# Two transformer blocks on one core: norms tile by tile over both halves, and first pieces summed with the feature tile outermost

## What is computed

```python
def rmsnorm(x, g):
    y = xf * lax.rsqrt(jnp.mean(xf * xf, axis=-1, keepdims=True) + EPS)
    return (y * g).astype(x.dtype)
def adaln(x, g, shift, scale):
    return rmsnorm(x, g) * (1 + scale) + shift
...
h = _rmsnorm(x, mix_norm_even[i]);  h @ w_in_even[i]
hx = adaln(x, norm1_g[layer], mod_x[0], mod_x[1]); hc = adaln(ctx, norm1_g[layer], mod_c[0], mod_c[1])
... hx @ w_in; hc @ w_in ...
swiglu(h, w1, w3, w2) = (silu(h @ w1) * (h @ w3)) @ w2
```

## Time and profile before

| what | value |
|---|---|
| median of 3 runs | 2679.54 us (2677.87 to 2680.28) |
| the profiled execution | 2674.07 us, its span 2672.2 us |
| PE busy | 2491.3 us, 93% of the span |
| DVE, ACT, POOL busy | 62%, 48%, 20% |
| mean granted PE clock | 0.957 of full speed |
| HBM traffic | 187 GB/s over the span |

### The profile page before, as it was taken

How to read it: one execution, slowest core, us unless ns; L and a number is a source line. 1 busy time by engine, 2 the same in 40 slices (tenths; PEclk the granted TensorE clock), 3 DMA queues, 4 the chain that set the end, 5 groups by cost and what they waited for, 6 DMA issues and landing times.

```text
span 2672.2 us, 37399 instructions
## 1 busy us (share of the span) xinstructions
PE 2491.3 (93%) x14331; PEld 2069.9 (77%) x14354; DVE 1665.4 (62%) x1755; ACT 1278.5 (48%) x1539; POOL 530.9 (20%) x406
## 2 busy tenths in 40 slices
PE   6989999999999998788999988888999999999997
PEld 4656999767999775567888977577887887887886
DVE  4635774545774676644222246656888888888886
ACT  4434443534443435523222124444677677677674
POOL 1001551101450200004000540001322322322321
PEclk9969999999999998699999999988999999999999
DMA  5464564454555220011222213104899899899894
GB/s 208 176 219 179 190 221 147 173 194 166 205 205 170 95 79 9 0 63 65 101 102 96 95 45 121 40 32 164 335 349 353 325 349 351 327 347 354 323 362 186
DMA packets 71328, 502.75 MB, mean 188 GB/s; under 512 B 8176, under 2 KB 8688, under 8 KB 11248
## 3 DMA queue, kind: packets, MB, share of 16 engines
q1 hardware_dynamic: 70128, 496.75, 50.7%
q0 software_dynamic: 1024, 3.61, 0.4%
HBM read 499.28 MB, written 1.05 MB: 187 GB/s over the span
## 4 chain that ended last, share of the span: by engine, by line
PE 84%; DVE 8%; ACT 5%; issue 1%; POOL 1%; DMA 1%; DVEq 0%; ACTq 0%; SPq 0%; PEldq 0%
PE ps L408 81%; DVE h L2047 1%; DVE ring_r L2069 1%; ACT ring_hi L1442 1%; POOL h_r L1332 1%; DVE h L2045 1%; DVE areaA L2039 1%; PE ps L448 1%; PE ps L1156 1%; ACT h L1520 1%; DVE areaB L2549 0%; ACT extra_r L1580 0%; DVE h L2049 0%; DVE temp L2132 0%; DMA areaB<-in_consts 0%
## 5 line engine op out<-in xcount | busy, mean ns | idle before, releaser
L1442 ACT ACTIVATE ring_hi<-ring 128x2048 fp32r<-128x2048 f32 x427 | 807.4, 1893 | 512.4 <-PE ps L408 507.4
L2799 DVE TENSOR_TENSOR ring_r<-ring,ring_hi 128x2048 fp32r<-128x2048 f32 x264 | 625.1, 2373 | 118.5 <-ACT ring_hi L1442 116.6
L408 PE MATMUL ps<-ring_hi,extra_r 128*128 128x512 f32 (+2 forms) x1808 | 609.4, 393 | 26.8 <-POOL h_r L1332 14.0
L2069 DVE TENSOR_TENSOR ring_r<-ring,ring_hi 128x2048 fp32r<-128x2048 f32 (+3 forms) x163 | 387.9, 2380 | 216.3 <-ACT ring_hi L1442 202.2
L408 PE MATMUL ps<-extra_r,ring_hi 128*128 128x256 f32 (+1 forms) x1432 | 465.5, 325 | 33.4 <-POOL h_r L1332 20.1
L408 PE MATMUL ps<-h_r,ring_hi 128*128 128x256 f32 (+1 forms) x1432 | 459.5, 321 | 0.0
L408 PE MATMUL ps<-extra_r,ring_r 128*128 128x256 f32 (+1 forms) x1432 | 459.2, 321 | 0.0
L408 PE MATMUL ps<-ring_r,extra_r 128*128 128x512 f32 (+2 forms) x1104 | 426.0, 386 | 0.0
L408 PEld LDWEIGHTS ps<-ring_hi,extra_r 128*128 128x128 f32 x1808 | 342.9, 190 | 102.9 <-POOL h_r L1332 18.3
L408 PEld LDWEIGHTS ps<-extra_r,ring_hi 128*128 128x128 f32 x1432 | 275.2, 192 | 58.4 <-POOL h_r L1332 23.4
L408 PEld LDWEIGHTS ps<-h_r,ring_hi 128*128 128x128 f32 x1432 | 275.4, 192 | 18.9
(11 more groups left out here) (350 smaller groups left out, 3364.1 us busy)
## 6 DMA issues: line engine op xcount, KB each, us to landing
ring<-in_experts SPq DMA_DIRECT2D x264, 1024.0 KB, 4.9
ring<-in_stream SPq DMA_DIRECT2D x202, 1024.0 KB, 4.9
ring<-in_stream SPq DMA_DIRECT2D x6, 512.0 KB, 3.6
areaB<-in_consts POOLq DMA_DIRECT2D x3, 512.0 KB, 4.1
ring<-in_stream SPq DMA_DIRECT2D x2, 576.0 KB, 3.9
res<-in_xT SPq DMA_DIRECT2D x1, 1024.0 KB, 8.2
res<-in_ctxT POOLq DMA_DIRECT2D x1, 1024.0 KB, 7.3
out_xT<-h SPq DMA_DIRECT2D x4, 256.0 KB, 2.2
```

Of the source, the lines that this page charges most:

```text
L408: return pe.matmul(o, l, r, start=start, stop=stop, skip_group_check=True)
L1442: return act.activation(dst, src, ACT.Copy)
L2069: L.tell(TTN(ring_lo[:, s, 0:n], ring[:, s, 0:n], ring_hi[:, j % HIS, 0:n].bitcast(F32), ALU.subtract), "weights_lo")
L2799: TTN(ring_lo[:, s, :], ring[:, s, :], ring_hi[:, j % HIS, :].bitcast(F32), ALU.subtract).then_inc(sig("weights_lo"), 1)
```

## The change

Four things are changed.

1. `norm` takes the reciprocal half by half, each just before the half's first tile. With a shift the first group has one tile, the next three, the last four.
2. In in0 and ffn2 (`paired`) the tiles are made feature by feature: tile 0 of half 0, tile 0 of half 1, tile 1 of half 0, and so on, on DVE, ACT and POOL alike.
3. In `tokens` and `project` the first unit's pieces are summed with the feature tile outermost and the token tile inside.
4. In `ffn` pieces 0 and 1 are taken together, and summed with the feature tile outermost: per tile piece 0's two products, then piece 1's. The other pieces go as before; with one half, they sum product a = 0 over all tiles, then a = 1.

```diff
+        def by_tile(n, paired=False):
+            if paired:
+                return [(hf, k) for k in range(KD) for hf in range(n)]
+            return [(hf, k) for hf in range(n) for k in range(KD)]
...
-                pe.wait_ge(sig("h_lo"), h_tiles[0] + hf * KD + k + 1)
+                pe.wait_ge(sig("h_lo"), h_tiles[0] + h_order.index((hf, k)) + 1)
...
-                        for x, t in enumerate(tiles):
-                            if half == 0:
+                        each = [(x, k) for x in range(len(tiles)) for k in range(4)]
+                        if first and j == 0:
+                            each = [(x, k) for k in range(4) for x in range(len(tiles))]
+                        for x, k in each:
...
-                h_split(halves)
-                for m0 in range(KF):
+                h_split(halves, halves == 2)
+
+                def weights(m0):
+                    src = [Piece(*w, 0, D, c0 + m0 * P, c0 + (m0 + 1) * P) for w, c0 in (wa, wb)]
+                    return split_chunk(src, "p (k a c) -> p k a c", k=8, a=2)
+
+                def up(v, u, a, k):
+                    if halves == 1:
+                        return mm3(ps[:, u.bank, a * T:(a + 1) * T], lambda s: v[s][:, k, a, :],
+                                   lambda s: hs[s][:, 0, k, :], k == 0 and a == 0, k == KD - 1)
+                    return mm3(ps[:, u.bank, :], lambda s: v[s][:, k, a, :], lambda s: hs[s][:, 0:2, k, :],
+                               k == 0, k == KD - 1)
+
+                def banks(m0):
+                    if halves == 1:
+                        return [take(tag, "up", m0, bank=m0 % 4)] * 2
+                    return [take(tag, "up", m0, a, bank=2 * (m0 % 2) + a) for a in range(2)]
+
+                vs = [weights(m0) for m0 in range(2)]
+                us = [banks(m0) for m0 in range(2)]
+                for k in range(KD):
+                    for m0 in range(2):
+                        for a in range(2):
+                            if m0 == 0 and a == 0:
+                                wait_h(halves - 1, k, us[0][0])
+                            m = up(vs[m0], us[m0][a], a, k)
+                            if k == KD - 1 and (a == 1 or halves == 2):
+                                full(m, us[m0][a])
+                for m0 in range(2):
+                    chunks[m0 - 2][2] = (bank_full[us[m0][1].bank], us[m0][1].nth + 1)
+                for m0 in range(2, KF):
                     each(m0)
...
+                    v, u = weights(m0), banks(m0)
+                    for a in range(2):
                         for k in range(KD):
+                            m = up(v, u[a], a, k)
+                        if a == 1 or halves == 2:
+                            full(m, u[a])
+                    release_with(u[1])
...
-                S(dve.reciprocal(rs, rs))
-
-                for i in range(n * KD):
-                    hf, k = divmod(i, KD)
+
+                for hf, k in by_tile(n, paired):
+                    if k == 0:
+                        S(dve.reciprocal(rs[:, hf * T:(hf + 1) * T], rs[:, hf * T:(hf + 1) * T]))
                     if shift:
-                        if k % 4 == 0:
-                            S(TTN(h[:, hf, k:k + 4, :], res[:, hf, k:k + 4, :],
-                                  bc(rs[:, hf * T:(hf + 1) * T], 1, [P, 4, T]), ALU.mult))
+                        if k in (0, 1, 4):
+                            m = (1, 3, 0, 0, 4)[k]
+                            S(TTN(h[:, hf, k:k + m, :], res[:, hf, k:k + m, :],
+                                  bc(rs[:, hf * T:(hf + 1) * T], 1, [P, m, T]), ALU.mult))
...
-                norm(2, lambda hf, k: gated(l, 1, hf, k), lambda hf, k: gated(l, 0, hf, k), split=True)
+                norm(2, lambda hf, k: gated(l, 1, hf, k), lambda hf, k: gated(l, 0, hf, k), split=True,
+                     paired=l == 0)
...
-                norm(nh, lambda hf, k: gated(l, 4, hf, k), lambda hf, k: gated(l, 3, hf, k), split=True)
+                norm(nh, lambda hf, k: gated(l, 4, hf, k), lambda hf, k: gated(l, 3, hf, k), split=True, paired=l == 0)
```

More of the change, by code:

```diff
@@ L465, in project @@
                         v = split_chunk(Piece(*w, half * 512, (half + 1) * 512, a, b), "p (k c) -> p k c", k=4)
-                        for x, t in enumerate(tiles):
-                            if half == 0:
-                                us.append(take(tag, j, t))
[L469 to L476, removed]
+                        each = [(x, k) for x in range(len(tiles)) for k in range(4)]
+                        if first and j == 0:
+                            each = [(x, k) for k in range(4) for x in range(len(tiles))]
+                        for x, k in each:
+                            t, kk = tiles[x], 4 * half + k
+                            if kk == 0:
+                                us.append(take(tag, j, t))
+                            if first and j == 0:
+                                wait_h(t // 2, kk, us[x])
+                            m = mm3(ps[:, us[x].bank, 0:b - a],
+                                    lambda s: hs[s][:, t // 2, kk, (t % 2) * P:(t % 2) * P + P],
+                                    lambda s: v[s][:, k, :], kk == 0, kk == KD - 1)
+                            if kk == KD - 1:
                                 full(m, us[x])
@@ L497, in tokens @@
                     v = split_chunk(Piece(*w, half * 512, (half + 1) * 512, a, b), "p (k c) -> p k c", k=4)
-                    for t in range(TT):
-                        if half == 0:
-                            us.append(take(tag, i, t))
[L501 to L507, removed]
+                    each = [(t, k) for t in range(TT) for k in range(4)]
+                    if i == 0:
+                        each = [(t, k) for k in range(4) for t in range(TT)]
+                    for t, k in each:
+                        kk = 4 * half + k
+                        if kk == 0:
+                            us.append(take(tag, i, t))
+                        if i == 0:
+                            wait_h(0, kk, us[t])
+                        m = mm3(ps[:, us[t].bank, 0:b - a], lambda s: hs[s][:, 0, kk, t * P:(t + 1) * P],
+                                lambda s: v[s][:, k, :], kk == 0, kk == KD - 1)
+                        if kk == KD - 1:
                             full(m, us[t])
@@ L1550, in hi_upto, with h_rounded @@
                     his[0] += 1
-            def h_rounded(n):
-                for i in range(n * KD):
-                    hf, k = divmod(i, KD)
+            def h_rounded(n, paired=False):
+                for i, (hf, k) in enumerate(by_tile(n, paired)):
                     L.wait("h_raw", rounded[0] + i + 1)
@@ L2033, in _, with norm @@
             norms = [0]
-            def norm(n, gain, shift=None, name="h_ready", split=False):
+            def norm(n, gain, shift=None, name="h_ready", split=False, paired=False):
                 norms[0] += 1
```

23 lines of the change are left out of this document (10 added, 13 removed).

## The result

The median rose from 2678.7 to 2713.39 us, each of four runs: a ratio of 1.0134, with an interval of 1.0107 to 1.016. The profiled execution took 2715.0 us with a span of 2713.2; that of before had 2672.2 (the earlier trace rows are its chain). So the two spans lie 41.0 us apart and the medians 34.7.

What follows compares the result with a forecast made beforehand. It took PE to bound the kernel, with 84% of the span. Terms of 12.9, 11.2, 13.2, 2.4 and 0.7 us sum to 40.4; on 2674.07 that gives 2714.5, with 5.5 kept for the median 2720; range 2703 to 2735.

Steps and rivals of the forecast that it cites:

- part 1: Dense stages: PE waits for the second piece's split behind the norm; ffn0 +12.9, ffn1 +11.2, ffn2 +13.2 us.
- the second wait: Dense stages, behind the pair: PE idles until DVE has split piece 2, 3.3 us in ffn0.
- The second cold start: Dense stages, start of piece 2: low clock after the new idle stretch, put at 1.6 us each.
- sum of 40.4: Whole kernel: all predicted slowdowns added, 12.9 + 11.2 + 13.2 + 2.4 + 0.7 us.
- part 2: Norms by halves, first group of one tile: in0 +2.4 us, in1 +0.7, router norm 0.
- The +0.8: Norms over both halves: extra group operations and split reciprocals make each 0.8 us longer.
- forecast of 3.1: in0 and in1: a longer norm in both and a cold start in in0, +2.4 and +0.7 us.
- Part 3: Token projections' first units, reordered sums: cost 0, bounds 0 and 1 us in each of three stages.
- (a): Rival: in the dense stages the pair starts on the first tile after all; -4.9 us, 2675 us; 4%.
- (b): Rival: dense stages wait at the pair's start but not for piece 2's split; +25 us, 2705 us; 8%.
- (c): Rival: longer low clock or late piece 3, 3 to 5 us more per dense stage; +52, 2731 us; 13%.
- (d): The forecast itself, for the whole kernel: +40 us, 75%.

Runs made afterwards that it cites:

- split_first: The changed kernel with DVE's split of the second dense piece moved ahead of the norm: 2683.27 us, 1.0005.
- warm_ahead: The changed kernel with the dense stages' warm-up matmuls moved ahead of PE's wait for the splits, as many as fill it: 2705.80 us, 1.0098.
- dense_only: The kernel before with the new ffn alone, pieces 0 and 1 taken together, feature tile outermost: 2715.18 us, 1.0148.
- tokens_only: The kernel before with only the new project and token loops, first units summed feature tile outermost: 2681.41 us, 1.0006.
- third_split: The changed kernel with the second dense piece's split ahead of the norm, the third's right behind it, later roundings and splits one piece earlier: 2662.95 us, 0.994.
- norm_only: The changed kernel with the old ffn, project and token loops, keeping the new norms and tile order: 2682.09 us, 1.0018.

## Why the prediction was right, and where it was off

**The second piece's split holds the pair (part 1).** Shown, by the two timelines and by split_first, in which that split alone was moved and the loss went. The pair's start was put 14.9 us behind the norm's start (275.3 - 260.41; the terms 271.41 and 3.8 give 275.2, so 14.8); it came at 280.04 - 265.14 = 14.90. The split ended 10.93 us behind the norm's start where 11.00 was taken, and from there to the pair it was 3.97 us (280.04 - 276.07, of which 0.48 lie ahead of the warm-ups) where 3.8 was taken.

**The pair and the second wait.** The pair was put at 11.5 us and took 12.2 (280.04 to 295.60 - 3.36 = 292.24), since the sum took the rate of matmuls in full flow: the first two were still at the low clock (0.77 us for the first), and the end of the last one comes on top. Bank, convolution and split came as said. Piece 2 starts 30.46 us behind the norm's start, against 29.7 in the sum: 0.8 short. ffn1 was 1.1 short the same way (30.66 against 29.5), ffn2 0.6 (53.48 against 52.92), and there the sum had 0.8 for a longer norm that didn't come, so its other terms were 1.4 short.

**The second cold start.** This is the mis-sized term. It was put at 1.6; after loses 2.8 us there by the window, and some 3.0 and 2.7 in ffn1 and ffn2:

```profile
701.00:708.00 7.00, 6.46 (x32) 6.46 (x33) 5.16 (x6) 4.21 (x3) 3.28 (x2) 0.54 0.44 185
...
1275.00:1283.00 8.00, 7.39 (x22) 5.87 (x23) 3.66 (x3) 0.92 (x1) 6.03 (x3) 0.63 0.26 110
```

(0.46 of 7.00 and 0.37 of 8.00 us are 3.2 and 3.0; half of the 0.5 and 0.6 us in which PE was still idle at the start of each window comes off.) With the delay of piece 2's start the stages close: in ffn0 30.46 us behind the norm's start against 278.89 - 260.41 = 18.48 before, +12.0, and 2.8 make 14.8, as measured; in ffn1 +10.7 and 3.0 make 13.7 against 13.6; in ffn2 +12.2 and 2.7 make 14.9 against 15.0. The same wait was followed by a loss of only 1.5 to 1.6 us in warm_ahead, and dense_only's ffn0 (+12.9) lies on the forecast. So 1.6 is within what occurs. How often the longer loss comes in ordinary executions no run here says: only profiled executions have windows.

**Where the sum was lucky.** The sum of 40.4 lies 0.6 from the 41.0 between the profiled executions, and that is two misses of opposite sign: the three dense stages were put at 37.3 and came to 43.4, all else was put at +3.1 and came to -2.3. The median was then put at 2720 by keeping the 5.5 us by which before's median lay above its profiled execution. That distance did not come again: after's median lies 1.6 us below its profiled execution, and the medians differ by 34.7.

**The norm over both halves (part 2).** The +0.8 is wrong. From the first reciprocal to the split behind the norm, before took 888.67 - 868.31 = 20.36 us in in0, and after 918.56 - 898.34 = 20.22. DVE's timeline of after, in0:

```profile
900.13 0.42 DVE L2071 TENSOR_TENSOR h<-res,areaA 128x256 f32<-128x256 f32 x1
...
903.73 0.96 DVE L2071 TENSOR_TENSOR h<-res,areaA 128x768 f32<-128x768 f32 x1
...
918.56 5.78 DVE L2095 TENSOR_TENSOR ring_r<-ring,ring_hi 128x2048 fp32r<-128x2048 f32 x3
```

In ffn2 it is the same, 20.03 us before and 19.94 after. The op durations, 0.42 and 0.96, are those of the sum. What the sum left out is that the same op can take longer beside POOL (the earlier trace rows have 1.22 and 1.64 for it); with the tiles started sooner, fewer of them may meet POOL. That last is argued from those rows, not isolated. The Trainium skill, "VectorE: DVE Perf Modes", section on the TRN2 errata, was weighed there against splitting ops: the fixed latency per op that it states is there in these rows (0.42 and 0.96, 1.38 in sum, for 1.22), and it did not decide.

**in0 and in1.** PE's wait in in0 came out at 3.94 us for 0.71, as said, and the cold start behind it is there: PEclk 0.68 from 921 to 925. Yet the stretch is 2.0 shorter, not 2.4 longer. Without the 0.8 of the norm, 1.6 was due, and the scatter of such a stretch is larger than that, so these runs can't tell. In in1 PE waited 11.3 us instead of 7.58 at the same split, since it had its tiles sooner, and the stretch didn't grow. The forecast of 3.1 for both is not confirmed.

**Part 3.** Put at 0 with up to 1 us in each of three stages; tokens_only's ratio of 1.0006 is 1.6 us, with an interval that holds 0.

**The rivals.** (a), the pair starting on the first tile, was decided by what it named, weights_lo against the first h_lo: split_first makes it true. Its price came out at 1.0005, within no change; its sum had -4.9. ffn2 alone, -3.9 for -6.5, is near it; ffn0 and ffn1 came 2.1 us above its 0 and -1.5, for which the 1.7 us of low clock behind the second wait, left out of that sum, is nearly enough. (b), no second wait, is refuted by 3.36, 3.37 and 4.14 us. In ffn2 this wait hides another: the bank came free 0.8 us behind the pair's end, so with the split in time a wait of at least that length would have stayed, and third_split showed it. (c), 3 to 5 us more in each dense stage, didn't come: the stages lie 1.9, 2.4 and 1.8 above the forecast, by the clock and the pair's end and not by piece 3, at which PE shows no wait in any of the three. (d) holds: +34.7 on the medians, +41.0 between profiled executions, for +40.4.

## What to carry over

Before an engine is made to consume two prepared pieces together, look up where the preparation of the second stands in the other engine's queue: here one split of 2.6 us behind a norm cost 12.7 to 18.9 us in each stage (after less split_first, profiled executions), and a change worth some 4.5 us, or 9.5 with its banks, showed as 35 lost. When that is mended, ask what the pair fills or empties together (here the banks) and move that too. Here warm-up matmuls behind the last wait took 4.04 us and ran wholly at the low clock; ahead of it they cost nothing, and the pair started 3.9 us sooner.

## What the runs showed of the hardware

- The same idle stretch of 3.37 us on PE, at the same place, was followed by a loss of 1.5 to 1.6 us of clock in warm_ahead and of 2.8 to 3.0 in after. A gap of 1.75 us was followed by full clock in before's ffn0 and by half clock (0.66 over 5 us) in before's ffn1 and norm_only's ffn0. Which comes can't be read from the gap's length. The Trainium skill, "TensorE: Matmul & The Clock Gate", section "Why this matters for your kernels", has the gaps send PE to half clock, and the rows agree in that, with the one of before's ffn0 as an exception.
- Ten bf16 warm-ups take 2.1 to 2.3 us at full clock, 4.04 us after 10.52 us of idle time in after, the whole of them at 0.50, and 3.62 us after 10.14 in dense_only.
- In the first attention stage both kernels are mostly at the low clock from 151 us on. In before it ends by 196 us; in after it is 0.50 from 195 to 209 us with PE busy 13.78 of 14 us, in code that is the same. Stretches with attention scatter by 3 to 5 us for this. The dense ones repeat to 0.03 us where the clock takes the same course, and differ by 1.5 to 1.9 us where it doesn't.
